# Regrouping the weight slots of two experts in the paired phases of a mixture-of-experts layer

## The reference, cut to what matters

```python
def moe_swiglu(h, w_router, w_gu, w_down):      # D = 1024, 8 experts, FFN_EXPERT = 3584
    def fn(t):
        ...
        act = jax.nn.silu(gu[..., :FFN_EXPERT]) * gu[..., FFN_EXPERT:] * gate[..., None]
        return jnp.einsum('nef,efd->nd', act, w_down)
```

## Time and profile before

| | us |
|---|---|
| median of 3 runs | 1363.53 (1360.8 to 1365.19) |
| the profiled execution | 1363.06 |
| its span | 1361.3 |
| TensorE busy | 1320.7 (97%) |
| VectorE busy | 763.7 (56%) |
| ScalarE busy | 643.4 (47%) |

### The profile page before, as it was taken

One profiled execution on the slowest core, in us unless ns is written; L12 is line 12 of the kernel. 1 busy time (PEld: TensorE's weight loads), 2 busy tenths in 40 slices (PEclk: granted clock), 3 DMA queues, 4 the chain that ended last, 5 costly groups with the idle time before them and its releaser, 6 DMA issues.

```text
span 1361.3 us, 18942 instructions
## 1 busy us (share of the span) xinstructions
PE 1320.7 (97%) x7610; PEld 1002.3 (74%) x7610; DVE 763.7 (56%) x912; ACT 643.4 (47%) x771; POOL 31.3 (2%) x96
## 2 busy tenths in 40 slices
PE   7999999998999988999999999999999999999997
PEld 7987888887987677777776666777666777666762
DVE  6855645544647557973367635367645357654332
ACT  5646544434456546662356533356534255644221
POOL 5000000001000000000000000000000000000000
PEclk9999999999999898999999999999999999999999
DMA  8543555555452127899999999999999999999996
GB/s 355 171 170 105 204 186 186 185 185 185 156 217 80 45 85 264 332 363 429 427 427 427 424 414 426 428 426 428 428 417 425 427 427 428 427 418 424 428 428 275
DMA packets 36086, 431.67 MB, mean 317 GB/s; under 512 B 4000, under 2 KB 4000, under 8 KB 5152
## 3 DMA queue, kind: packets, MB, share of 16 engines
q1 hardware_dynamic: 35856, 429.94, 78.3%
q10 hardware_dynamic: 144, 0.52, 0.1%
HBM read 429.40 MB, written 1.05 MB: 316 GB/s over the span
## 4 chain that ended last, share of the span: by engine, by line
PE 90%; DVE 4%; ACT 2%; DMA 2%; issue 1%; POOL 0%; POOLq 0%; SPq 0%; DVEq 0%; ACTq 0%
PE bank L1602 20%; PE bank L1604 19%; PE bank L1603 19%; PE bank L2171 13%; PE bank L2192 7%; PE bank L1988 1%; DMA raw<-in_moe 1%; PE bank L2121 1%; PE bank L2218 1%; PE bank L1972 1%; DVE w_lo L1507 1%; PE bank L1928 1%; PE bank L2229 1%; DVE ht_lo L1027 1%; PE bank L1890 1%
## 5 line engine op out<-in xcount | busy, mean ns | idle before, releaser
L1507 DVE TENSOR_TENSOR w_lo<-raw,w_hi 128x2048 fp32r<-128x2048 f32 x114 | 257.9, 2287 | 151.2 <-ACT w_hi L902 150.9
L1602 PE MATMUL bank<-w_hi,ht_hi 128*128 128x512 f32 (+1 forms) x768 | 304.3, 396 | 3.3 <-DVE ht_lo L1305 1.1
L1604 PE MATMUL bank<-w_hi,ht_lo 128*128 128x512 f32 (+1 forms) x768 | 296.6, 386 | 0.0
L902 ACT ACTIVATE w_hi<-raw 128x2048 fp32r<-128x2048 f32 x114 | 214.3, 1909 | 135.2 <-DMA raw<-in_moe 120.5
L1003 DVE TENSOR_TENSOR w_lo<-raw,w_hi 128x2048 fp32r<-128x2048 f32 x70 | 159.6, 2288 | 112.3 <-ACT w_hi L592 112.3
L1603 PE MATMUL bank<-w_lo,ht_hi 128*128 128x512 f32 (+1 forms) x568 | 218.2, 384 | 0.0
L1602 PEld LDWEIGHTS bank<-w_hi,ht_hi 128*128 128x128 f32 x768 | 144.5, 188 | 48.0 <-issue 17.8
L592 ACT ACTIVATE w_hi<-raw 128x2048 fp32r<-128x2048 f32 x71 | 135.5, 1918 | 90.8 <-PE bank L1604 88.9
L1604 PEld LDWEIGHTS bank<-w_hi,ht_lo 128*128 128x128 f32 x768 | 144.4, 188 | 30.1
L1507 DVE TENSOR_TENSOR more_lo<-more,w_hi 128x2048 fp32r<-128x2048 f32 x50 | 114.1, 2289 | 80.6 <-ACT w_hi L902 80.5
L902 ACT ACTIVATE w_hi<-more 128x2048 fp32r<-128x2048 f32 x50 | 95.9, 1918 | 101.4 <-DMA more<-in_moe 54.3
(11 more groups left out here) (325 smaller groups left out, 1510.3 us busy)
## 6 DMA issues: line engine op xcount, KB each, us to landing
raw<-in_moe SPq DMA_DIRECT2D x112, 2048.0 KB, 13.1
more<-in_moe SPq DMA_DIRECT2D x54, 2048.0 KB, 12.9
raw<-in_wts SPq DMA_DIRECT2D x71, 1024.0 KB, 4.8
more<-in_moe SPq DMA_DIRECT2D x4, 1024.0 KB, 14.7
xs<-in_x SPq DMA_DIRECT2D x2, 512.0 KB, 3.9
out<-xn SPq DMA_DIRECT2D x4, 256.0 KB, 2.0
pk<-in_packed SPq DMA_DIRECT2D x1, 517.0 KB, 7.6
g1b<-in_norm_ffn ACTq DMA_DIRECT2D x1, 512.0 KB, 3.5
```

The source lines that it names most:

```text
L902: a(w_hi[:, hi_order(n) % SPLIT, :], slot_raw(n), ACT.Copy).then_inc(s_hi, 1)
L1507: v.tensor_tensor(slot_lo(n), slot_raw(n), w_hi[:, hi_order(n) % SPLIT, :].bitcast(F32), ALU.subtract).then_inc(s_lo, 1)
L1602: mm(out_, sh, mh, start=first, stop=False)
L1604: return mm(out_, sl, mh, start=False, stop=last)
```

## The change

In paired phases positions are dealt out differently. Chunk 0 keeps 4 up slots and 2 down slots (positions 0 to 5). After that chunks go in pairs (1 and 2, 3 and 4, 5 and 6): 8 up slots, then 4 down slots, so positions 6 to 17, 18 to 29, 30 to 41, with the down slots at 14 to 17, 26 to 29, 38 to 41. The loads, the splitting and TensorE all follow the new numbers. The number of loads, splits, matmuls and transposes is the same. In P2 the limit of the splitting becomes `last + 4` (SPLIT) in place of `last + 5`; in P1 it stays `last + 5`.

```diff
+    def downs_before(s):
+
+        if s < 6:
+            return max(s - 4, 0)
+        group, at = divmod(s - 6, 12)
+        return 2 + 4 * group + max(at - 8, 0)
 ...
-        return N0 - 4 + UP_SLOTS + r * JOB_SLOTS + 2 * (b // 6) + max(b % 6 - 4, 0) + 4 * (d // 6) + min(d % 6, 4)
+        return N0 - 4 + UP_SLOTS + r * JOB_SLOTS + downs_before(b) + d - downs_before(d)
 ...
     def up_slot(c, h, u, paired):
 
-        return (6 if paired else 4) * c + 2 * h + u
+        if not paired:
+            return 4 * c + 2 * h + u
+        group, odd = divmod(c + 1, 2)
+        return (12 * group - 6 + 4 * odd if c else 0) + 2 * h + u
 ...
     def down_slot(d, paired):
-        return 6 * (d // 2) + 4 + d % 2 if paired else d
+        if not paired:
+            return d
+        group, at = divmod(d + 2, 4)
+        return 12 * group + 2 + at if d >= 2 else 4 + d
+
+    def downs_after(c):
+
+        return () if c % 2 else (c - 1, c) if c else (0,)
 ...
 # SyncE, phase_loads
-                if up is None and c == DOWN_SLOTS // 2 - 1:
+                    for b in downs_after(c):
+                        load_pair(n, job_pair(bass.ds(down, 1), UP_SLOTS + 2 * b), i)
+                        n += 2
+                    continue
+                if c == DOWN_SLOTS // 2 - 1:
 ...
 # ScalarE and VectorE, the limit of the splitting
-                split(min(last + MOE_AHEAD, length + 1) if paired else last + AHEAD)
+                split(min(last + (MOE_AHEAD if up else SPLIT), length + 1) if paired else last + AHEAD)
 ...
 # TensorE
-                    for d in (2 * c, 2 * c + 1):
+                    for d in [2 * b + j for b in downs_after(c) for j in range(2)]:
                         down_part(i, first + down_slot(d, paired), d, down)
```

## The result

The changed kernel takes **1388.29 us** (median of 4 runs, 1386.28 to 1392.84) against 1364.36 (4 runs, 1360.8 to 1365.19) for the kernel before in the same session: ratio 1.0185, 95% interval 1.0154 to 1.0217. It is slower, by 1.5 to 2.2%. The profiled execution took 1388.05, its span is 1386.3, so 25.0 more than the 1361.3 of before.

The account below looks back on a forecast made before the run. TensorE was taken as the bound, by a little, with the loads close behind. Terms 15.5 + 6.9 - 5.2 - 2.2 + 1.4 = +16.4 on the profiled 1363.1 gave 1379.5 us; own range 1370 to 1387, wide range 1366 to 1391.

Parts of the forecast that it names:

- first rival: Clock falls at most of eight TensorE waits, seven more than counted at 1.4 us each: 1389 us; chance 0.17.
- waits for the product: In P1, chunk 6's second half waits for product_b, queued behind a slot not yet landed: plus 15.5 us.
- border waits: At three P1 to P2 borders, TensorE waits 2.3 us for position 1's late w_lo: plus 6.9 us.
- fewer changes in P2: Three B down blocks merge in each of three P2, saving 0.33 us each: minus 3.0 us.
- fewer changes in P1: Three merges in each of four P1 save 0.18 us each at the A block: minus 2.2 us.
- old waits gone: The last P1's old waits for w_lo, 0.5 and 1.7 us, are replaced by the new ones: minus 2.2 us.
- clock: One fall of TensorE's clock to 1.2 GHz, after the wait of about 4 us in the last P1: plus 1.4 us.
- it meets an empty queue and lands 8.0 after the release: Later P1: the load of positions 6 and 7 finds nothing queued ahead, landing 8.0 us after its release.
- P2's close call: Position 13's w_lo before chunk 1's product_a leaves 0.3 to 0.5 us: no cost, or 0.5 at nine places.
- second rival: Loads keep their landings because the queue does not run empty, so only the first P1 waits fully: 1367.9 us; chance 0.10.
- Its sign: Deciding test for loads keeping their landings: whether positions 6 and 7 of P1 still land over 8 us after release.
- The third: Not slower: neither product nor position 1 late, 1362.6 us; needs position 38 landed before 682.5 in the first P1; chance 0.08.

Follow-up runs that it names:

- e6: The kernel before with only P2 grouped as in the change, P1 in the old order with its old limit; 1364.24 us, ratio 1.0002.
- e3: The changed kernel with its new order kept and both P1 limits mended (last + 4, and position 43 in the last step); 1366.87 us, ratio 1.0025.
- e4: The kernel before with only the splitting limit of the last step of P1 lowered from 43 to 42; 1373.83 us, ratio 1.0065.
- e2: The changed kernel with the splitting limit in P1 lowered from last + 5 to last + 4 in all steps but the last; 1372.26 us, ratio 1.0062.
- e7: The kernel before with only P1 grouped as in the change, both P1 limits mended, P2 in the old order; 1364.27 us, ratio 1.0001.
- e8: The changed kernel with each slot loaded by its own 1 MiB transfer once its own place is released; 1377.36 us, ratio 1.0094.
- e5: The kernel before with only the splitting limit in P2 lowered from last + 5 to last + 4; 1365.25 us, ratio 1.0005.
- e1: The changed kernel with the splitting limit of the last step of P1 put back to position 43; 1375.75 us, ratio 1.0096.
- e10: The kernel before with every load of the rounds held back until two more slots are released; 1378.67 us in a single run.

## Why the prediction held

1379.5 was forecast, 1388.3 came: the direction, the two waits and their places are as predicted, the size is 9 us short. The time lies above the forecast's own range (1370 to 1387) and only in the wide one (to 1391), whose upper end was made for the first rival's clock falls. Two of the terms that came out too small, the landings and the changes in P1, have no part in that upper end, so it is partly luck that the wide range holds the time. From scatter to scatter a round takes 215.2 and 214.6 us, where some 211 was said and 207.5 was before. By its own terms, in the profiled executions:

| term | forecast | measured |
|---|---|---|
| waits for the product | +15.5 | +17.3 (2.35, 4.8, 4.1, 6.0 in the four P1) |
| border waits | +6.9 | +7.5 |
| fewer changes in P2 | -3.0 | -3.3 |
| fewer changes in P1 | -2.2 | -0.4 |
| old waits gone | -2.2 | -2.2 |
| clock | +1.4 | +6.4 (four falls of 1.6) |
| sum | +16.4 | +25.3; the first B matmul of the first P1 starts 0.35 earlier, so the span grows by 25.0 |

**The bound.** Right: TensorE by a little, with the transfers close behind. e6 shows how close: all of P2's gain was lost again at the loads, as the "hardly more than 0.5 us" of the first part said. It fits that e3, without either of the two added waits, gains nothing.

**The border wait.** Right in place, cause and price (2.35 against 2.3; 2.5 with the slower first steps). e4 shows it alone.

**The wait for the product.** Right in cause; e2 shows it. For the first P1 the sum took the landing 0.5 late and the product at landing + 4.7 (4.62 came), and 2.35 us were lost against 3.0. In the second the step that failed is "it meets an empty queue and lands 8.0 after the release". SyncE's timeline shows that the queue was short, but not empty:

```profile
805.48 0.33 SPq L441 DMA_DIRECT2D raw<-in_moe  x1
811.37 0.33 SPq L441 DMA_DIRECT2D more<-in_moe  x1
```

The pair of positions 6 and 7 was issued at 811.37, 0.2 after its release, with one pair ahead of it that landed at 814.97; it landed at 820.75, 9.6 after the release, and position 38 at 900.17, 16 pairs and 79.4 us later, as forecast. In the third P1 the same pair took 10.0 from its issue. That is 1.6 to 2.2 us more than I took, and the second and third P1 lost 1.8 and 1.1 more than forecast; in the third a clock fall came on top. A pair's landing was neither "issue + 7.7" nor "landing ahead + 4.9" but later than both (819.1 and 819.9 here). In the last P1 the waits are 6.0 against 6.5, and the larger one, 3.41 of idle time, came at chunk 4 and not at chunk 6. The clock fell there, and 1.5 us of slow matmuls then stand ahead of chunk 6, which waits so much less.

That holds for both falls in P1, and the sum above hides it. When half 1 of chunk 6 may start is set by the landing of position 38, late or not: in the third P1 it landed at 1116.19, the product was done at 1120.85 and the half started at 1120.98. The fall in chunk 4 only used up what chunk 6 would have waited. With these falls in them the four P1 are 2.35, 4.8, 5.8 and 7.5 us late, 20.5 together, against 15.5: the mis-sized term is the landing, and of the falls only the two at the borders (3.2) are a cost of their own. The sum per phase held better than the places.

**The changes in P2.** Right: PE timeline of after, one merged block.

```profile
748.49 0.39 PE L1625 MATMUL bank<-w_hi,ht_lo 128*128 128x512 f32 x1
748.81 7.09 PE L2213 MATMUL bank<-raw,at_b 128*64 128x512 f32 x32
```

The four slots take 6.92 to the next instruction (two blocks of 3.58 before), a P2 107.65 in place of 108.75.

**The changes in P1.** Wrong. The merged A block saves 0.21 (11.00 us where the two were 5.56 and 5.65), but the transpose of each odd chunk's product is now followed by B matmuls, where it used to be followed by A matmuls. Both cases on PE in after:

```profile
683.95 0.44 PE L2250 MATMUL bank<-ident,avb 128*128 128x128 f32 x2
684.32 1.95 PE L2192 MATMUL bank<-raw,xb 128*64 128x256 f32 x16
```

```profile
693.21 0.44 PE L2250 MATMUL bank<-ident,avb 128*128 128x128 f32 x2
693.40 0.48 PE L1623 MATMUL bank<-w_hi,at_hi 128*128 128x512 f32 x1
```

It takes 0.37 to the first B matmul and 0.19 to the first A matmul. These 0.18 take back nearly what a merge gives: 0.03 is left of each, 0.09 of the three in a phase, as in e7. The sum counted changes between A and B and left out the transpose that stands between them.

**The clock.** The first rival was partly right. It priced a fall at 1.4 and put eight of them; there were four of 1.6, after two borders and two product waits. I counted one, from one row. The time is close to that rival's 1389, but not by its reason: three falls more than counted are 5 us and not its 10, and by the landings only two of them lengthened the whole. Over the four kernels with border waits of 2.2 us (after, e2, e4, e8) the clock fell after 7 of 12, so a wait of this length is about as likely to bring a fall as not: the forecast's eight waits of 2 us and more should have been counted with some four falls, not one. After idle times under 2.1 us in these phases no profile here shows a fall; in e3 an idle time of 3.34 passed without one, in e7 one of 2.35.

**P2's close call** did not bite: no wait in P2 in after, and e5 shows the limit free.

**The second rival** (the loads keep their landings) is out: position 38 of the second P1 landed at 900.17, not at 893.8, and the loads lost 29.3 us in place of 7.3. Its sign came true all the same: positions 6 and 7 landed over 8 us after their release. The sign was badly chosen, since a queue that is not empty doesn't mean landings that stay. **The third** is out by the two waits and by its own point: position 38 of the first P1 landed at 684.96, and 682.5 was needed.

**What stays open.** e3 measures 3.5 us above before, e6 and e7, its two halves, 0.3 and 0.1. From the first P1 to the last scatter e3's profiled execution takes 743.81 us and that of before 743.60, so its profile does not show the difference; its profiled run, 1364.66, is also the fastest of its eight. Its wait of 3.34 us may bring a clock fall in other runs, which would be 1.6; that was not seen. Why a short queue loses time is open too: the runs show that a late release is enough to bring it, not what the transfers do meanwhile. No version here beats the kernel before.

## What to carry to other kernels

When a regrouping changes which slot stands ahead of an instruction in an in-order queue, go through every limit that counts slots: work that prepares a slot k places ahead must not stand before a result that is already due, and a limit that was safe because those k places held slots of another kind is not safe after the regrouping. Where the ring of loads is full, a wait of the consumer can be paid more than once (the border: 12.5 us in e1 for 7.5 of waits), since it delays the releases and so the landings a ring later; mend the wait before judging the order. And a gain on the busiest engine counts only as far as the last transfer's landing lets it.

## What was not expected of the hardware

- **A short queue loses time before it is empty.** Averages by how long before the landing ahead of it a 2 MiB pair was issued, in after: 2 to 3 us, 6.35 from landing to landing (3 pairs); 3 to 4 us, 5.98 (13); 4 to 5 us, 5.20 (16); 5 and more, 4.9. e10, in the old order, gives 5.82 at 3 to 4 us (6), 5.10 at 4 to 5 (15) and one of 8.71 at 2 to 3. The Trainium skill, DMA: Bandwidth & Descriptors, "Anatomy of one DMA", gives a transfer that GpSimd issues a fixed part of about 2.0 us beside the time of its bytes. The loads here are issued by SyncE and show more: 7.7 us with little ahead, less the 4.9 at pace, is 2.8; the 1 MiB loads ahead of the experts, most with nothing in front of them, take 4.8 (median), less 2.5 is 2.3. The lead that hides it is some 5 us. So the trace doesn't bear out the 2.0 for these loads, and the prediction's sentence on it left out that the figure is for another path.
- **The size of a transfer shows at the full rate**: transfers of 1 MiB each run at 421 GB/s, those of 2 MiB at 427 (e8 against after, middle slices). That is 4.97 us against 4.893 for the same 2 MiB.
- **The clock can fall after 2.2 us of idle time on TensorE** with dense work on both sides, and did in 7 of 12 cases, at 1.6 us each.
- **A B matmul behind a transpose** starts 0.37 us after the transpose's start, an A matmul 0.19.
